# Router logits taken from the raw residual beside the output projection, and roots ahead of the first modulation, in a two-layer mixture-of-experts trunk on one Trainium2 core

## The chip, the core and the metric

The kernel runs on one core of a Trainium2 chip (trn2). The metric is the device time of one execution in microseconds, less is better. Three runs of the kernel before are shown, and one execution was profiled.

## The reference

Two layers work on 384 tokens of 1024 features (128 context tokens of one request, 256 latent tokens of another), all in float32. Cut to what the change touches, each layer computes:

```python
sh1, sc1, gt1, sh2, sc2, gt2 = ada_mod(cond, w_ada[l], b_ada[l])   # silu(cond) @ w_ada + b_ada, per request
h = rms_norm(y, g_attn[l]) * (1 + sc1) + sh1                       # first modulation
...                                                               # three attention groups on h @ w_in
y = y + gt1 * (o @ w_out[l])                                       # output projection, residual y
h = rms_norm(y, g_ffn[l]) * (1 + sc2) + sh2                        # second modulation
scores = sigmoid(h @ w_router)                                     # 16 experts in 4 groups
# best group by the sum of its top 2 of scores + b_router, top 2 experts inside it, weights normalised
y = y + gt2 * moe(h, ...)                                          # gate, up, silu, down for the chosen experts
```

`rms_norm(y, g)` is y times its root 1/sqrt(mean(y*y) + 1e-6), times g. The root is one number per token, so `h @ w_router` equals root * (y @ (g (1+sc2) w_router)) + sh2 @ w_router. `cond` is one vector for the context tokens and one for the latent tokens, so gain and shift have two sets of columns.

## The kernel before

The five engines each run one hand-written program (TensorE from line 724, ScalarE from 1163, VectorE from 1438, GpSimd from 1887, the SyncE transfers from 578); semaphores join them. The residual lies transposed in `zT` (features on partitions, 8 blocks k of 384 tokens), the modulated input in `hT`. Products are float32, and each shows in the trace as two matmul records. PSUM has 8 banks: six go round for "jobs" in the order of `job_order` (L156), bank 7 (`bN`) holds the sums of squares, banks 6 and 7 the attention outputs.

**Order of the work around the change, layer 0 start.** TensorE turns the input rows, adds the squares with 48 records of one column (`piece_sums`, L736), and goes on to the four adaLN chunks of the first modulation (`ada`, L787: a job A is a product of 32 columns wide tiles over a 2 MB weight chunk, L795, a job B turns the row that ScalarE copied out, L802). Beside that, VectorE works out the root by three Newton steps (`rsqrt`, L1465). Then TensorE spreads the root over a bank (`spread`, L763, job n1b), and VectorE normalises: for each block k one product with the spread root (L1521), and for odd k the modulation too (L1516); ScalarE modulates the even blocks (`modulate`, L1196, record L1202). The projection cq0 (L829) waits for each block in turn (`h_ready`, L751), and all products of the layer follow.

**The end of attention.** The output projection has eight jobs op0 to op7 of 8 products each (`proj`, L807, record L813), queued without a gap. VectorE adds each to the residual (L1677), ScalarE squares it (L1194), VectorE adds the squares (L1671). Then TensorE runs job A of the first of the chunks in `ADA_ROUTE[l]` (four in layer 0, two in layer 1), the sums (L748), A of the second, B of the first, the spread of the root (job n2b), and the router: 8 products of 32 columns wide tiles, each waiting for its block of `hT` (L1006). ScalarE copies the logits out, TensorE turns them (L1013), VectorE reduces them (L1720), ScalarE takes the exponential (L1331), and VectorE chooses group and experts in a chain of small operations (L1723 to L1732, ends with `s_mask`), then works out weights (L1737 to L1749). TensorE turns `hT` back into rows (jobs hr00 to hr21, L1009 and L1017, record L733), ScalarE copies them out and stores them to `hscr` (L1336), runs jobs A and B of the chunks that are left, waits for `s_mask`, and ranks the tokens (L1024 to L1030). VectorE reads the rank (L1752), makes one-hot matrices (L1782), TensorE makes slots with them (L1046), GpSimd gathers rows of `hscr` (L1970), and the experts begin.

In layer 0 two chunks stand behind the turns (A and B of the third around the mask, the fourth behind the rank, L1032), in layer 1 only one job B.

**The experts.** Each of 16 takes three 2 MB weight chunks from a ring of six slots; SyncE loads a slot when its last reader is done (L661).

Of the kernel before, what the change touches and what calls it, by code (L numbers as in the profile page):

```python
# [15 lines left out]
P = 128  # L16
# [139 lines left out]
def job_order():  # L156

    order = ["vecA", "vecB"] + [f"x{t}{h}" for t in range(NT) for h in range(2)]
    for l in range(DEPTH):
        n = (ada_jobs(ADA_FIRST) if l == 0 else []) + ["n1b"] + (BETWEEN_SPREAD if l else [])  # L160
        n += ["cq0"] + (BETWEEN_FIRST if l else []) + ["cq1"] + [f"nav{t}" for t in range(NT)] + ["ckv", "kpe", "swk"] + [f"swv{t}" for t in range(NT)]
        n += ["nqc", "naq0", "nkc", "naq1", "nqb", "nak0", "nkb", "nak1", "rkp", "swq0", "cache1", "cache2", "swq1", "swq2"]
        n += ["mq0", "mq1", "mq2", "mq3", "rm0", "mq4", "mq5", "rm1", "mk0", "mk1", "rm2", "mk2", "mk3", "mk4", "mk5"]
        for i in range(NS + LAG_PV):
            if i < NS:
                n.append(f"S{i}")
            n += ENTRY.get(i, [])
# [12 lines left out]
    order += ["nfb"] + [f"fo{t}{h}" for h in range(2) for t in range(NT)]  # L180
    at, signalled, busy, where = 0, [0] * NB, [None] * NB, {}
    for j in order:
        wide = j[1] in PAIRED if type(j) is tuple else False
        if wide:
            at += at % 2
        b = at % NB
        taken = [b, b + 1] if wide else [b]
        before = {busy[k] for k in taken if busy[k] is not None}
        where[j] = (b, signalled[b], sorted(before))
        signalled[b] += 1  # L190
        for k in taken:
            busy[k] = (b, signalled[b])
        at += len(taken)
    return where
# [44 lines left out]
def build(nc, A, C_dram, O):  # L239
    with ExitStack() as ctx:  # L240
        def sb(name, shape, dt=F32):
            return ctx.enter_context(nc.sbuf_tensor(name, shape, dt))
# [35 lines left out]
        gcol = sb("gcol", [P, 2])  # L278
        wqb = sb("wqb", [P, 2, MH * QKD])
# [66 lines left out]
        wr32 = c3(carve(KT * 32), KT)  # L346
# [25 lines left out]
        bN = banks[7]  # L372
        bX, bG, bU, bA, bY = banks[0:2], banks[2], banks[3], banks[4], banks[5:7]
# [42 lines left out]
        s_wr = sem("s_wr")  # L416
        s_rexp = sem("s_rexp")
# [307 lines left out]
        def _(pe):  # L725
# [25 lines left out]
            def h_ready(l, which, k):  # L751

                pe.wait_ge((s_ha, s_hv)[k % 2], 4 * norm_no(l, which) + k // 2 + 1)
# [30 lines left out]
            pe.wait_ge(s_sil, 1)  # L784

            for l in range(DEPTH):
# [20 lines left out]
                def proj(name, w, c, m, first_after=None):  # L807

                    b = fill_begin((l, name))
                    for k in range(KT):  # L810
                        if first_after is not None:
                            h_ready(l, first_after, k)
                        last = mm(b[0:m, 0:T], w[:, k, c:c + m], hT[:, k, :], start=(k == 0), stop=(k == KT - 1))  # L813
                    filled((l, name), last)
# [14 lines left out]
                proj("cq0", w, NAH * HD, P, first_after=0)  # L829
# [169 lines left out]
                if l == 0:  # L999
                    pe.wait_ge(s_bs, 16 * 4)  # L1000

                pe.wait_ge(s_wr, 2 * (l + 1))
# [152 lines left out]
            for h in range(2):  # L1155
                if h == 0:
                    pe.wait_ge(s_hv, 4 * norm_no(DEPTH, 0) + 1)
                else:
                    read_out(pe, "nfb")
                for t in range(NT):  # L1160
                    turn4(f"fo{t}{h}", lambda k: hT[:, 4 * h + k, t * P:(t + 1) * P])

        @block.scalar
        def _(act):
# [31 lines left out]
            def modulate(l, which):  # L1196

                for k in range(0, KT, 2):
                    act.wait_ge(s_xn, 4 * norm_no(l, which) + k // 2 + 1)
                    for cond in range(2):  # L1200
                        x = hT[:, k, sel(cond)]
                        last = A_(x, x, ACT.Identity, bias=modT[:, l, 24 * which + k, cond:cond + 1],  # L1202
                                  scale=gain[:, which, k, cond:cond + 1])
                    last.then_inc(s_ha, 1)
# [11 lines left out]
            for l in range(DEPTH):  # L1216
# [4 lines left out]
                modulate(l, 0)  # L1221
# [217 lines left out]
        def _(v):  # L1439
# [62 lines left out]
            def gains(l, which):  # L1502
# [4 lines left out]
                chain(tt(gain[:, which], gain[:, which], g, ALU.mult))  # L1507

            def normalise(j, l, which):

                b = take(v, j)

                def modulate(k):
                    for cond in range(2):
                        x = hT[:, k, sel(cond)]
                        ins = ts(x, x, gain[:, which, k, cond:cond + 1], modT[:, l, 24 * which + k, cond:cond + 1],  # L1516
                                 ALU.mult, ALU.add)
                    ins.then_inc(s_hv, 1)

                for k in range(KT):  # L1520
# [8 lines left out]
                    if k % 2:  # L1529
                        modulate(k)  # L1530
# [10 lines left out]
            for l in range(DEPTH):  # L1541
# [4 lines left out]
                for j in ada_jobs(ADA_FIRST) if l == 0 else []:  # L1546
                    ada(l, j)

                v.wait_ge(s_mod, len(ADA_FIRST if l == 0 else ADA_FIRST + ADA_ATT))
                gains(l, 0)  # L1550
                normalise((l, "n1b"), l, 0)
# [120 lines left out]

                for n in range(KT):
# [9 lines left out]
                v.wait_ge(s_mod, ADA_ALL.index((0, 9) if l == 0 else (1, 7)) + 1)  # L1683
                gains(l, 1)
                add_squares(KT - 1)
                rsqrt((l, 1), D)
                for j in route[0:3]:
                    ada(l, j)
                normalise((l, "n2b"), l, 1)


# [23 lines left out]

                b = take(v, (l, "routerT"))
                if l + 1 < DEPTH:

                    v.wait_ge(s_bmw, 16 * (l + 2))
                evac((l, "routerT"), nc.vector.tensor_reduce(  # L1720
                    te(R[0]), b[:, 0:T].rearrange("p (t g r) -> p t r g", t=NT, g=4)[:, :, 0:NE, :], AX.X, ALU.add))
# [166 lines left out]
        def _(g):  # L1888
# [30 lines left out]
            for l in range(DEPTH):  # L1919
# [35 lines left out]
                nc.gpsimd.memset(wr32[:, :, NE:32], 0.0).then_inc(s_wr, 1)  # L1955
                nc.gpsimd.tensor_copy(wr32[:, :, 0:NE], wr[:]).then_inc(s_wr, 1)
# [64 lines left out]
```

## Time and profile before

| | |
|---|---|
| runs shown | 1251.38, 1252.31, 1255.2 us, median 1252.31 |
| profiled execution | 1255.41 us, its span 1253.4 us (2.01 us lie around the span) |
| mean granted TensorE clock of the profiled execution | 0.947 |
| TensorE busy | 1152.9 us, 92% of the span |
| VectorE, ScalarE, GpSimd busy | 772.4, 632.9, 127.8 us |
| moved by DMA | 314.35 MB, mean 251 GB/s |

A row of the timeline gives the start in us from the span's start, the time it took, engine, line of the kernel, operation, output<-input with shapes, and a count; in brackets stands how long the engine was idle before and what released it. PEld is the weight load of TensorE. A row of a table by stage gives, for a stretch, its length and each engine's busy time and number of records in it, the granted clock (1.00 is the full clock), the busy share of the DMA engines and what they moved. In a chain row stand start, length and what lay on the chain.

### The profile page before, as it was taken

The numbers are of one execution on the slowest core, as the hardware profiler recorded it, in microseconds if no ns is written. First come the engines' busy times: TensorE is split into PE (matmuls) and PEld (weight loads), VectorE is DVE, ScalarE is ACT, GpSimd is POOL, SyncE is SP. The second block draws the span as 40 slices with busy tenths as digits, with TensorE's granted clock in tenths as the row PEclk, the third lists the DMA queues.
The fourth block names the chain that finished last, engine by engine and source line by source line (L and its number), as shares of the span: only waits on it lengthen the run. The fifth ranks groups of instructions, "written<-read, shape, count | busy, mean of one in ns | idle before, by whom it ended". The sixth has DMA issues, their size and how long they took to land.

```text
span 1253.4 us, 14864 instructions
## 1 busy us (share of the span) xinstructions
PE 1152.9 (92%) x5574; PEld 844.6 (67%) x5574; DVE 772.4 (62%) x1056; ACT 632.9 (50%) x751; POOL 127.8 (10%) x157
## 2 busy tenths in 40 slices
PE   6999998897899999999879998889789999999956
PEld 5576354554788888888666754455578888888846
DVE  1312356427698888888451233742768888988845
ACT  2201455315377777777320035631447777777721
POOL 2241100310100101010010011000000101010000
PEclk9899999999799999999969998999779999999985
DMA  9994478339489999999699140002549999999621
GB/s 330 335 309 169 145 264 280 100 109 377 148 321 372 359 376 366 383 375 367 221 345 240 68 168 16 1 1 81 245 158 352 369 375 378 377 364 369 257 87 75
DMA packets 81257, 314.35 MB, mean 251 GB/s; under 512 B 22766, under 2 KB 27100, under 8 KB 68396
## 3 DMA queue, kind: packets, MB, share of 16 engines
q1 hardware_dynamic: 65548, 279.17, 61.2%
q0 software_dynamic: 13152, 24.96, 6.0%
q10 hardware_dynamic: 2496, 9.44, 2.0%
q8 instruction: 35, 0.57, 0.2%
q14 instruction: 26, 0.21, 0.1%
HBM read 308.11 MB, written 26.38 MB: 267 GB/s over the span
## 4 chain that ended last, share of the span: by engine, by line
PE 84%; DVE 7%; issue 3%; ACT 3%; DMA 2%; SPq 0%; ACTq 0%; POOL 0%; POOLq 0%; DVEq 0%
PE bank L813 17%; PE bank L1072 14%; PE bank L1066 14%; PE bank L1067 14%; PE bank L795 3%; PE bank L941 3%; PE bank L820 3%; PE bank L740 2%; PE bank L1056 2%; PE bank L955 2%; ACT work L1295 2%; PE bank L733 2%; PE bank L973 1%; PE bank L1046 1%; PE bank L874 1%
## 5 line engine op out<-in xcount | busy, mean ns | idle before, releaser
L1791 DVE TENSOR_TENSOR ring_r<-ring,work_r 128x4096 fp32r<-128x4096 f32 x96 | 421.6, 4416 | 0.1
L1352 ACT ACTIVATE work_r<-ring 128x4096 fp32r<-128x4096 f32 x96 | 349.6, 3644 | 138.0 <-PE bank L1067 104.4
L1066 PE MATMUL bank<-work_r 128*128 128x512 f32 x768 | 310.1, 404 | 12.3 <-issue 5.1
L1067 PE MATMUL bank<-work_r 128*128 128x512 f32 x768 | 303.9, 396 | 0.0
L813 PE MATMUL bank<-hT,ring 128*128 128x384 f32 (+1 forms) x640 | 213.7, 493 | 3.3 <-ACT hT L1202 1.9
L1072 PE MATMUL bank<-ring_r,work_r 128*128 128x512 f32 x768 | 195.1, 396 | 0.4 <-DVE ring_r L1791 0.4
L813 PEld LDWEIGHTS bank<-hT,ring 128*128 128x128 f32 (+1 forms) x640 | 121.5, 192 | 88.0 <-issue 11.6
L1066 PEld LDWEIGHTS bank<-work_r 128*128 128x128 f32 x768 | 147.5, 192 | 43.9 <-issue 5.8
L1072 PEld LDWEIGHTS bank<-ring_r,work_r 128*128 128x128 f32 x768 | 144.2, 188 | 34.5 <-DVE ring_r L1791 0.8
L1067 PEld LDWEIGHTS bank<-work_r 128*128 128x128 f32 x768 | 147.1, 192 | 29.6
L1174 ACT ACTIVATE work<-bank 128x384 f32<-128x384 f32 (+6 forms) x79 | 38.0, 494 | 179.7 <-PE bank L813 89.3
L1970 POOL DMA_INDIRECT work<-hscr,idxg x32 | 32.8, 1026 | 402.7 <-PE bank L1056 260.9
L1625 DVE TENSOR_REDUCE st<-bank 128x2 f32<-128x768 f32 (+1 forms) x48 | 37.4, 778 | 50.3 <-PE bank L941 40.6
L1977 POOL DMA_INDIRECT yscr<-work,idxs x32 | 32.1, 1004 | 276.5 <-ACT work L1378 276.5
L795 PE MATMUL bank<-ring,sil 128*32 128x512 f32 x384 | 50.8, 655 | 7.4 <-ACT work L1295 5.6
L1796 DVE TENSOR_TENSOR work_r<-bank,work_r 128x512 fp32r<-128x512 f32 x64 | 41.2, 685 | 26.6 <-ACT work_r L1359 26.6
L1295 ACT ACTIVATE work<-bank,st 128x384 f32<-128x384 f32 (+1 forms) x96 | 47.9, 506 | 17.3 <-DVE st L1625 9.5
L1677 DVE SCALAR_TENSOR_TENSOR zT<-bank,modT,zT 128x256 f32<-128x256 f32 (+1 forms) x32 | 11.9, 413 | 67.9 <-PE bank L813 67.9
L941 PE MATMUL bank<-work 64*128 64x384 f32 (+3 forms) x192 | 48.0, 467 | 6.1 <-ACT work L1295 4.7
L1194 ACT ACTIVATE work<-zT 128x384 f32<-128x384 f32 x16 | 8.4, 523 | 80.6 <-DVE zT L1677 80.6
L955 PE MATMUL bank<-cst,work 128*128 128x128 f32 x224 | 35.2, 288 | 12.3 <-ACT work L1295 8.9
L1810 DVE TENSOR_TENSOR work_r<-bank,work_r 128x512 fp32r<-128x512 f32 x32 | 22.1, 691 | 37.8 <-ACT work_r L1371 37.8
(202 smaller groups left out, 1152.7 us busy)
## 6 DMA issues: line engine op xcount, KB each, us to landing
ring<-in_w_gate SPq DMA_DIRECT2D x32, 2048.0 KB, 11.5
ring<-in_w_up SPq DMA_DIRECT2D x32, 2048.0 KB, 12.3
ring<-in_w_down SPq DMA_DIRECT2D x32, 2048.0 KB, 12.3
ring<-in_w_ada SPq DMA_DIRECT2D x24, 2048.0 KB, 10.0
ring<-in_w_in SPq DMA_DIRECT2D x4, 2048.0 KB, 15.5
work<-yscr ACTq DMA_DIRECT2D x6, 1024.0 KB, 7.1
ring<-in_w_out SPq DMA_DIRECT2D x4, 1280.0 KB, 8.0
ring<-in_w_in SPq DMA_DIRECT2D x12, 256.0 KB, 6.9
```

The source lines that it names most:

```text
L795: last = mm(b[32 * (k % 4):32 * (k % 4) + 32, :], sil32[:, k, :], w[:, k, :], start=(k < 4), stop=(k >= 4), skip_group_check=True)
L813: last = mm(b[0:m, 0:T], w[:, k, c:c + m], hT[:, k, :], start=(k == 0), stop=(k == KT - 1))
L941: last = mm(b[:, s, 0:n], lhs, rhs, start=True, stop=True)
L955: last = turn_(b[:, s, c * P:(c + 1) * P], pr[(2 * i + s) % 6][:, c * P:(c + 1) * P], ident)
L1066: mm(b[:], x_hi[:, k, :], hi[:, k, half, :], start=(k == 0), stop=False)
L1067: last = mm(b[:], x_lo[:, k, :], hi[:, k, half, :], start=False, stop=False)
L1072: last = mm(b[:], x_hi[:, k, :], lo[:, k, half, :], start=False, stop=(k == nk - 1))
L1174: evac(j, A_(dst, src, ACT.Copy, scale=scale))
L1295: ins = A_(pr[(2 * i + s) % 6][:, 0:n], b[:, s], ACT.Exp, bias=st[:, r, 0, s:s + 1], accum_out=st[:, r, 1, s:s + 1])
L1352: A_(w_hi[:, slot % 2, :], ring[slot][:], ACT.Copy).then_inc(s_hi, 1)
L1791: tt(ring_r[slot][:], ring[slot][:], w_hi[:, slot % 2, :].bitcast(F32), ALU.subtract).then_inc(s_lo, 1)
L1796: ins = tt(xs_lo[:, 4 * h:4 * h + 4, :], bX[h][:].rearrange("p (k s) -> p k s", k=4), xs_hi[:, 4 * h:4 * h + 4, :].bitcast(F32), ALU.subtract)
```

## The change

The first spread of layer 0 moves ahead of its four adaLN chunks; VectorE multiplies all eight blocks by the spread root then, and modulation alone is left for after the chunks. In each layer, gain 2 is worked out before the output projection, two weight sets `wz` (gain times router weights, one per condition) are made by VectorE, and TensorE accumulates `wz` times the raw residual block n-1 behind job op n, the last one behind the first adaLN product. Eight tiny products of the shift with the router weights (`wb`) give a bias, which ScalarE adds when it copies the logits out. VectorE multiplies by the root after the turn and the reduction. ScalarE modulates all eight blocks of the second modulation, VectorE only normalises them; the turn of the logits moves ahead of B of the first chunk and of the spread, and all six turns of `hT` come behind.

```diff
 job_order:
-        n = (ada_jobs(ADA_FIRST) if l == 0 else []) + ["n1b"] + (BETWEEN_SPREAD if l else [])
+        n = ["n1b"] + (BETWEEN_SPREAD if l else ada_jobs(ADA_FIRST))
-        n += r[0:3] + ["n2b", "router", "hr00", "routerT"] + [f"hr{t}{h}" for t in range(NT) for h in range(2)][1:]
+        n += r[0:2] + ["routerT"] + r[2:3] + ["n2b"] + [f"hr{t}{h}" for t in range(NT) for h in range(2)]
 TensorE:
-            pe.wait_ge(s_sil, 1)
...
-                for j in ada_jobs(ADA_FIRST) if l == 0 else []:
-                    ada(j)
                 spread((l, "n1b"), roots_before(l, 0) + 1)
-                for j in BETWEEN_SPREAD if l else []:
+                if l == 0:
+                    pe.wait_ge(s_sil, 1)
+                for j in BETWEEN_SPREAD if l else ada_jobs(ADA_FIRST):
                     ada(j)
...
+                def router_part(k):
+                    read_out(pe, (l, f"op{k}"))
+                    for cond in range(2):
+                        c = sel(cond)
+                        last = mm(bR[32 * (k % 4):32 * (k % 4) + 32, c], wz[:, k, cond, :], zT[:, k, c], start=(k < 4 and cond == 0), stop=(k >= 4),
+                                  skip_group_check=True)
+                    return last
                 for n in range(KT):
...
                     proj(f"op{n}", w, (n % 4) * P, P)
+                    if n == 0:
+                        if l == 0:
+                            pe.wait_ge(s_bs, 16 * 4)
+                        pe.wait_ge(s_wr, 3 * (l + 1))
+                        for k in range(KT):
+                            last = mm(bN[32 * (k % 4):32 * (k % 4) + 32, 8:10], wb[:, k, :], modT[:, l, 24 + k, :], start=(k < 4),
+                                      stop=(k >= 4), skip_group_check=True)
+                        last.then_inc(s_router, 1)
+                        pe.wait_ge(s_wz, l + 1)
+                    else:
+                        router_part(n - 1)
                 for j in route[0:1]:
                     ada(j)
+                router_part(KT - 1).then_inc(s_router, 1)
+                pe.wait_ge(s_rlog, 2 * l + 1)
                 sums_of_added(l)
-                for j in route[1:3]:
+                for j in route[1:2]:
                     ada(j)
-                spread((l, "n2b"), roots_before(l, 1) + 1)
...
-                b = fill_begin((l, "router"))
-                for k in range(KT):
-                    h_ready(l, 1, k)
-                    last = mm(b[32 * (k % 4):32 * (k % 4) + 32, 0:T], wr32[:, k, :], hT[:, k, :], start=(k < 4), stop=(k >= 4),
-                              skip_group_check=True)
-                filled((l, "router"), last)
-                turn4((l, "hr00"), lambda k: hT[:, k, 0:P])
-                read_out(pe, (l, "router"))
+                pe.wait_ge(s_rlog, 2 * (l + 1))
                 b = fill_begin((l, "routerT"))
...
-                for i in range(1, 2 * NT):
+                for j in route[2:3]:
+                    ada(j)
+                spread((l, "n2b"), roots_before(l, 1) + 1)
+                for i in range(2 * NT):
                     t, h = divmod(i, 2)
+                    pe.wait_ge(s_ha, (4 + KT) * l + 4 + 4 * (h + 1))
                     turn4((l, f"hr{t}{h}"), lambda k: hT[:, 4 * h + k, t * P:(t + 1) * P])
 ScalarE:
+                act.wait_ge(s_router, 2 * l + 1)
+                A_(rbias[:], bN[:, 8:10], ACT.Copy).then_inc(s_rlog, 1)
                 squares_behind_out(l)
-                for j in route[0:3]:
+                for j in route[0:1]:
                     ada_row(l, j)
-                modulate(l, 1)
...
-                copy((l, "router"), rlog, T)
-                read_out(act, (l, "routerT"))
+                act.wait_ge(s_router, 2 * l + 2)
+                for cond in range(2):
+                    last = A_(rlog[:, sel(cond)], bR[:, sel(cond)], ACT.Identity, bias=rbias[:, cond:cond + 1])
+                last.then_inc(s_rlog, 1)
+                for j in route[1:3]:
+                    ada_row(l, j)
+                act.wait_ge(s_logit, l + 1)
                 A_(rw[:, 0, :], rw[:, 0, :], ACT.Exp, scale=-1.0).then_inc(s_rexp, 1)
+                modulate_all(l)
 VectorE, layer 0 start:
+                    normalise_first((l, "n1b"))
+                    for j in ada_jobs(ADA_FIRST):
+                        ada(l, j)
+                    v.wait_ge(s_mod, len(ADA_FIRST))
+                    gains(l, 0).then_inc(s_xn, 4)
+                    v.wait_ge(s_xn, 4)
+                    read_out(v, (l, "n1b"))
+                    for k in range(1, KT, 2):
+                        modulate(l, 0, k)
 VectorE, before op0:
+                chain(gains(l, 1))
+                v.wait_ge(s_bs, 16 * 4)
+                for cond in range(2):
+                    ins = tt(wz[:, :, cond, 0:NE], wr[:], gain[:, 1, :, cond].unsqueeze(2).to_broadcast([P, KT, NE]), ALU.mult)
+                ins.then_inc(s_wz, 1)
 VectorE, behind the root:
+                for j in route[0:2]:
+                    ada(l, j)
...
+                    both_parts, b[:, 0:T].rearrange("p (t g r) -> p t r g", t=NT, g=4), AX.X, ALU.add))
+                read_out(v, (l, "routerT"))
+                v.wait_ge(s_root, roots_before(l, 1) + 1)
+                chain(tt(te(R[0]), both_parts[:, :, 0:NE], ns[:, 1, :].unsqueeze(2).to_broadcast([P, NT, NE]), ALU.mult))
+                tt(te(R[0]), te(R[0]), both_parts[:, :, NE:2 * NE], ALU.add).then_inc(s_logit, 1)
+                for j in route[2:3]:
+                    ada(l, j)
+                normalise_second((l, "n2b"))
                 v.wait_ge(s_rexp, l + 1)
 GpSimd:
-                nc.gpsimd.memset(wr32[:, :, NE:32], 0.0).then_inc(s_wr, 1)
-                nc.gpsimd.tensor_copy(wr32[:, :, 0:NE], wr[:]).then_inc(s_wr, 1)
+                nc.gpsimd.memset(wz[:, :, :, NE:32], 0.0).then_inc(s_wr, 1)
+                nc.gpsimd.memset(wb[:, :, 0:NE], 0.0).then_inc(s_wr, 1)
+                nc.gpsimd.tensor_copy(wb[:, :, NE:32], wr[:]).then_inc(s_wr, 1)
```

`normalise_second` is eight products of `zT` and the spread root on VectorE, each released to ScalarE; `modulate_all` is the two modulations of each of the eight blocks on ScalarE; `modulate(l, 0, k)` on VectorE is the two of one odd block.

## Rows read from the trace of the kernel before

**Rows 1.** The page: the chain that ended last, shares of the span by engine.

```profile
PE 84%; DVE 7%; issue 3%; ACT 3%; DMA 2%; SPq 0%; ACTq 0%; POOL 0%; POOLq 0%; DVEq 0%
```

**Rows 2.** Table by stage: output projection of layer 1, idle ahead of rank, rank, start of cq0.

```profile
833.20:874.70 41.50, 41.48 (x128) 24.28 (x129) 7.52 (x19) 3.66 (x7) 0.49 (x2) 1.00 0.14 51
892.55:895.88 3.33, 0.00 (x0) 0.00 (x0) 2.92 (x14) 2.46 (x5) 0.00 (x0) 0.96 0.89 359
895.90:899.90 4.00, 4.00 (x18) 3.91 (x18) 3.62 (x16) 4.00 (x2) 0.00 (x0) 0.50 0.22 89
45.00:48.80 3.80, 3.80 (x7) 2.02 (x6) 2.77 (x8) 1.97 (x4) 0.00 (x0) 0.50 1.05 388
```

**Rows 3.** Timeline of the start of layer 0.

```profile
12.61 3.68 PE L733 MATMUL bank<-cst,work 128*128 128x128 f32 x16 [0.64 <-DMA work<-in_x_sample]
16.81 3.21 ACT L1185 ACTIVATE hT<-zT 128x512 f32<-128x512 f32 x6
17.49 10.40 PE L740 MATMUL bank<-cst,hT 128*128 128x1 f32 x48 [1.20 <-ACT hT L1185]
28.03 0.16 DVE L1473 TENSOR_SCALAR ns<-bank 128x3 f32<-128x3 f32 x1 [11.88 <-PE bank L740]
30.29 0.17 DVE L1485 SCALAR_TENSOR_TENSOR ns<-ns 128x3 f32<-128x3 f32 x1
39.68 0.66 PE L802 MATMUL bank<-cst,arow 128*128 128x128 f32 x4 [0.69 <-ACT arow L1174]
41.22 1.02 DVE L1521 TENSOR_TENSOR hT<-zT,bank 128x384 f32<-128x384 f32 x2
42.94 13.61 PE L813 MATMUL bank<-hT,ring 128*128 128x384 f32 x32 [1.93 <-ACT hT L1202]
```

**Rows 4.** The chain of waits at the start of layer 0.

```profile
27.89 5.64 PE bank L795 x32
33.53 0.59 PE bank L802 x4
34.12 1.85 PE bank L795 x16
```

**Rows 5.** Timeline of layer 1, from op7 to the first gather.

```profile
874.70 1.92 PE L795 MATMUL bank<-ring,sil 128*32 128x512 f32 x16
876.96 0.83 PE L748 MATMUL bank<-cst,work 128*128 128x1 f32 x6 [0.34 <-DVE work L1671]
880.30 0.93 PE L768 MATMUL bank<-cst,ns 128*128 128x128 f32 x6
889.74 2.35 PE L733 MATMUL bank<-cst,hT 128*128 128x128 f32 x20
890.61 0.19 DVE L1723 TENSOR_SCALAR work<-work 128x48 f32<-128x48 f32 x1 [0.31 <-ACT work L1331]
895.89 0.61 PE L1027 MATMUL bank<-work,cst 128*128 128x16 f32 x2 [3.37 <-DVE work L1732]
904.90 1.34 POOL L1970 DMA_INDIRECT work<-hscr,idxg  x1 [71.06 <-issue]
```

**Rows 6.** Timeline of layer 0: first job A, rank, first one-hot.

```profile
280.14 1.93 PE L795 MATMUL bank<-ring,sil 128*32 128x512 f32 x16
301.39 0.40 PE L1027 MATMUL bank<-work,cst 128*128 128x16 f32 x2 [1.37 <-DVE work L1732]
307.70 3.69 DVE L1782 TENSOR_TENSOR work_r<-cst,work 128x512 fp32r<-128x512 f32 x6
```

**Rows 7.** Timeline of ScalarE in layer 1: a modulated block, the last store of rows.

```profile
886.75 0.99 ACT L1202 ACTIVATE hT<-hT,modT,gain 128x256 f32<-128x256 f32 x2 [0.64 <-DVE hT L1521]
894.59 0.33 ACTq L1336 DMA_DIRECT2D hscr<-work  x1
```

**Rows 8.** Table by stage: 14 experts of layer 1.

```profile
943.26:1194.42 251.16, 251.16 (x1178) 208.78 (x1177) 220.79 (x113) 193.72 (x126) 26.25 (x26) 1.00 0.93 352
```

**Rows 9.** The line of the six stores to `hscr`: time from issue to landing.

```profile
DMA to landing us min/median/max: 2.7/3.6/11.0
```

More of the change, by code:

```diff
@@ L416, in build @@
         s_wr = sem("s_wr")
+        s_wz = sem("s_wz")
+        s_router = sem("s_router")
+        s_rlog = sem("s_rlog")
+        s_logit = sem("s_logit")
         s_rexp = sem("s_rexp")
@@ L749, in sums_of_added, with h_ready @@
                 last.then_inc(s_sum, 1)
-            def h_ready(l, which, k):
-                pe.wait_ge((s_ha, s_hv)[k % 2], 4 * norm_no(l, which) + k // 2 + 1)
+            def h_ready(l, k):
+                pe.wait_ge((s_ha, s_hv)[k % 2], ((4 + KT) * l, 4 * l)[k % 2] + k // 2 + 1)
             def sums(j, sq, nk):
@@ L805, in _, with proj @@
                 route = ada_jobs(ADA_ROUTE[l])
-                def proj(name, w, c, m, first_after=None):
+                def proj(name, w, c, m, paced=False):
                     b = fill_begin((l, name))
                     for k in range(KT):
-                        if first_after is not None:
-                            h_ready(l, first_after, k)
+                        if paced:
+                            h_ready(l, k)
                         last = mm(b[0:m, 0:T], w[:, k, c:c + m], hT[:, k, :], start=(k == 0), stop=(k == KT - 1))
@@ L1194, in squares_behind_out, with modulate_block, modulate_even, modulate_all @@
                     A_(sq_new[n % 2] if n else sq_sum, zT[:, n, :], ACT.Square).then_inc(s_sq, 1)
-            def modulate(l, which):
-                for k in range(0, KT, 2):
[L1199 to L1204, printed above, removed]
+            def modulate_block(l, which, k):
+                for cond in range(2):
+                    x = hT[:, k, sel(cond)]
+                    last = A_(x, x, ACT.Identity, bias=modT[:, l, 24 * which + k, cond:cond + 1],
+                              scale=gain[:, which, k, cond:cond + 1])
+                last.then_inc(s_ha, 1)
+            def modulate_even(l):
+                for k in range(0, KT, 2):
+                    act.wait_ge(s_xn, (4 + KT - 1) * l + k // 2 + 1)
+                    modulate_block(l, 0, k)
+            def modulate_all(l):
+                for k in range(KT):
+                    if k < KT - 1:
+                        act.wait_ge(s_xn, (4 + KT - 1) * l + 4 + k + 1)
+                    else:
+                        read_out(act, (l, "n2b"))
+                    modulate_block(l, 1, k)
             def ada_row(l, j):
@@ L1506, in gains, with modulate, normalise_first, normalise_second @@
                 chain(ts(gain[:, which], modT[:, l, 24 * which + 8:24 * which + 16, :], 1.0, None, ALU.add))
-                chain(tt(gain[:, which], gain[:, which], g, ALU.mult))
+                return tt(gain[:, which], gain[:, which], g, ALU.mult)
+            def modulate(l, which, k):
+                for cond in range(2):
+                    x = hT[:, k, sel(cond)]
+                    ins = ts(x, x, gain[:, which, k, cond:cond + 1], modT[:, l, 24 * which + k, cond:cond + 1],
+                             ALU.mult, ALU.add)
+                ins.then_inc(s_hv, 1)
+            def normalise_first(j):
+                b = take(v, j)
+                for k in range(KT):
+                    ins = tt(hT[:, k, :], zT[:, k, :], b[:, 0:T], ALU.mult)
+                evac(j, ins)
+            def normalise_second(j):
+                b = take(v, j)
+                for k in range(KT):
+                    ins = tt(hT[:, k, :], zT[:, k, :], b[:, 0:T], ALU.mult)
+                    if k < KT - 1:
+                        ins.then_inc(s_xn, 1)
+                evac(j, ins)
             def normalise(j, l, which):
                 b = take(v, j)
[L1513 to L1518, printed above, removed]
                 for k in range(KT):
@@ L1529, in normalise @@
                     if k % 2:
-                        modulate(k)
+                        modulate(l, which, k)
             def normalise_last(j):
@@ L1545, in _ @@
                     ada(l, j)
[L1546 to L1551, printed above, removed]
+                if l == 0:
+                    normalise_first((l, "n1b"))
[7 more added lines that the diff above has]
+                        modulate(l, 0, k)
+                else:
+                    v.wait_ge(s_mod, len(ADA_FIRST + ADA_ATT))
+                    chain(gains(l, 0))
+                    normalise((l, "n1b"), l, 0)
                 for i in range(2):
@@ L1671, in add_squares @@
                     tt(sq_sum, sq_sum, sq_new[n % 2], ALU.add).then_inc(s_sqadd, 1)
+                v.wait_ge(s_mod, ADA_ALL.index((0, 9) if l == 0 else (1, 7)) + 1)
+                chain(gains(l, 1))
+                v.wait_ge(s_bs, 16 * 4)
+                for cond in range(2):
+                    ins = tt(wz[:, :, cond, 0:NE], wr[:], gain[:, 1, :, cond].unsqueeze(2).to_broadcast([P, KT, NE]), ALU.mult)
+                ins.then_inc(s_wz, 1)
                 for n in range(KT):
```

21 lines of the change are left out of this document (8 added, 13 removed).

## The prediction

> **What bounds the kernel now.** I read the page's chain first, then tables by stage, then the timeline around the two places that the change touches. The chain is 84% TensorE [rows 1], so what counts is when TensorE is held back or given more. In the output projection it is busy 41.48 of 41.50 us, 128 records of 384 columns, 0.324 us each [rows 2]: whatever is put there is paid in full. In the experts it is busy all of 251.16 us [rows 8], so a late start of the experts is a late end. Between these lie the two latency-bound stretches: the start of layer 0 [rows 3, 4], and in each layer the stretch from op7 to the one-hot matrices [rows 5, 6], where the path hops from engine to engine. A time worked out for a stretch is counted from E, the end of op7, which before is 874.70 in layer 1 and 280.14 in layer 0.
>
> **Start of layer 0.** The root is moved ahead of four adaLN chunks. Before, TensorE leaves the sums at 27.89 [rows 3] and starts the first job A at once [rows 4], while VectorE needs 2.43 us for the root, from 28.03 to 30.46 [rows 3]. After, the spread stands ahead of the first A, so TensorE stands still until 30.52: +2.63 us. The spread itself (0.93 us warm [rows 5]) comes off nothing, because before it lay beside the wait for the last B's modulation; at the half rate seen there it is up to 1.4: +0.9 to +1.4. Behind the last B, the path to cq0 was 2.60 us, from 40.34 to 42.94 [rows 3]; it loses one normalising product of 0.55: −0.55. The other seven were already hidden: cq0 ran at the clock of 0.50 [rows 2], seven records in 3.8 us, 1.1 us a block, slower than ScalarE gives blocks out (0.99 for each second one [rows 7]), so that having all blocks normalised buys nothing more. The eight products (8 x 0.51 = 4.1 us [rows 3]) run beside the first two A jobs (5.64 us [rows 4]). Sum: +3.2, bounds +2.4 (the clock rises earlier because the spread comes first) and +4.
>
> **In the output projection.** Removed is the router behind the normalisation; it was paced by the blocks, not by its own time. Added are seven parts ahead of op7's end, each 2 conditions x 2 records over 256 and 128 columns. By the 0.324 us for 384 columns [rows 2] a part is 0.65 us of streaming. They use 32 columns of the array, and the neighbours use 128. No row shows a narrow product amid wide ones in this stage; the nearest are jobs A and B in turn. A (16 records of 512 columns, four tiles at once) would stream in 1.73 by the same rate and takes 1.85; B (4 of 128 columns) would in 0.43 and takes 0.59 [rows 4]. So a change of shape costs at most 0.12 to 0.16 us, a part 0.65 to 0.97; I take 0.8. The Trainium skill ("TensorEngine Tiling (Array Packing)", Key Properties) says that changing the tiling mode drains the array; it gives no time. If all of A's and B's excess is that, a part costs 0.97 and the forecast goes up by 2.4 us over both layers; without a drain it goes down by 2.1. The bias adds 16 records of two columns. Nearest is the sums row, six records in 0.83 [rows 5], 0.14 each with wide weights, thus at most 2.2; four tiles at a time it would be a quarter, 0.5: I take 1.0. The memsets of GpSimd and the two products for `wz` on VectorE come within op0 (16 records, 5.2 us) and cost nothing; were they late, the bias and the whole rest of the projection would stand behind them. Each part reads block n-1, which VectorE has added by then (it needs under 1 us of the 5.2). Per layer E moves by 7 x 0.8 + 1.0 = **+6.6 us**, bounds +5.0 and +9.0.
>
> **From op7 to the mask.** After, with rows 5 for the times: A to E+2.0, last part to 2.8, sums to 3.6 (squares were ready before), root to 6.1; on TensorE the second A to 5.6, ScalarE's two copies of the logits are done beside it, three turns to 6.1, B to 6.8, spread to 7.7. VectorE reduces and scales the logits before that, then normalises 8 x 0.51 = 4.1 us to E+11.8 and starts the chain of choices there. Before, it started at 890.61, E+15.9. This is the gain: −4.1, less than the 6.6 above. The chain takes 5.3 us (890.61 to 895.89), so the mask is there at E+17.1 instead of E+21.2.
>
> **What is late next.** The turns of `hT` stand on TensorE ahead of the rank, and now wait for ScalarE alone. It starts its first block at E+8.3. One block is 0.99 [rows 7]; in a stream ScalarE hides some of it (six squares in 3.21, 0.54 each, against 0.62 alone), so I take 0.9 for a block, bounds 0.85 and 0.99: done at E+15.5. hr00 needs four blocks, the other five need all. TensorE has then done nothing but four short records for 7.8 us. Before, an idle stretch of 3.33 us was enough for the clock to stand at 0.50 in the rank [rows 2]. A turn at the low rate is 0.23 (16 in 3.68 [rows 3]), at the full one 0.12 (20 in 2.35 [rows 5]). I take the low one: five turns of four are 4.6 us, to E+20.1.
> - Layer 1: one B (0.7) puts the rank at E+20.8 instead of E+21.2 (895.89−874.70), −0.4. VectorE's weights wait for the same B, so nothing there is sooner. All of the mask's gain is gone.
> - Layer 0: A and B lie between. A is 1.85 at full and 3.79 at half rate (5.64−1.85 [rows 4]), the clock rising somewhere in it: 2.8; with B 0.7 the rank starts at E+23.6 instead of E+21.25 (301.39−280.14 [rows 6]), +2.3. Behind the rank everything keeps its 6.3 us to the first one-hot (301.39 to 307.70).
>
> Stores to `hscr`: ScalarE copies behind the turns and issues the last at about E+20.7, before at E+19.9 [rows 7]. It may land 11 us later [rows 9]; the first gather is at E+30.2 in layer 1 [rows 5] where the landings are the shorter ones. Hidden, with 1 to 6 us to spare. SyncE's loads that wait for the moved A jobs come up to 3 us later in layer 0; their data is wanted by the second expert: nothing.
>
> **Sum:** 3.2 + 2 x 6.6 + 2.3 − 0.4 = **+18.3 us**. The profiled execution would go from 1255.41 to 1273.7; it lies 3.1 above the median 1252.31, and against that the forecast is **1270.6 us**.
>
> **Rivals.**
> - *Turns at the full clock.* hr00 and the light work keep the clock up, as the paced router did before. Turns end at E+17.9, rank at E+18.6 in layer 1 (−2.6) and E+20.5 in layer 0 (−0.8): 3.2 + 13.2 − 3.4 = +13.0, 1265.3. For it: the clock stayed up with a product pair in each 1.6 us; against: here are 4 and 3 us with nothing.
> - *The mask decides.* If ScalarE's blocks come at the pace of VectorE's (0.51), the turns are done before the mask, and each layer gains the whole 4.1: 3.2 + 13.2 − 8.2 = +8.2, 1260.5. Against: no row shows ScalarE that fast.
> - *The experts give it back* (not slower). If the weight stream bounds the experts and is not itself late, the delay of both layers up to the experts disappears, and only the start's 3.2 is left: 1255.5, within what counts as no change. The transfers are busy 0.93 at 352 GB/s there, TensorE 1.00 [rows 8]; it decides once the transfers are the busier of the two. Against: SyncE loads a slot only when TensorE has read it, so a late start is late for the stream too.
> - *Parts dearer*: 0.97 a part, 2.2 for the bias, gives E+9.0: 1275.4. It is the top of the forecast's own range.
> - *The change does not do what it says* would show as logits taken after normalisation; the program's order leaves no room for it.
>
> **Chances.** Forecast (with dear parts in it) 0.58, full clock 0.22, mask 0.08, experts 0.05; the rest is for things unseen, more of it above no change than below. The range takes in the first two and their bounds: from 1260 (full clock with parts of 0.65, 0.5 for the bias and +2.4 at the start: 1252.3+9.0, less 1 for a mask that decides in one layer) to 1278 (+4 at the start, E+9.0 twice, blocks of 0.99 and a slow A that put the ranks at +4.0 and +0.3: +26.3). A difference of under 0.3% (3.8 us) can't be told from none: slower 0.91, same 0.06, faster 0.03.
>
> **What would show it.** In the profile after: TensorE idle 2.6 us ahead of the spread at 27.9; cq0 starts near 46. The output projection takes 48 us instead of 41.5 up to the first A. VectorE starts the choices about 12 us behind op7 and 4 us sooner relative to it. ScalarE modulates without a pause for 7.2 us. The turns take 4.6 us at a clock of 0.50, and the rank's releaser is TensorE's own order, not VectorE's mask. It is wrong if a part takes under 0.4 us, if cq0 starts by 44, or if the experts' stage gets shorter.

## The result and the profile after

The changed kernel takes 1266.6 us (median of 4 runs, 1265.89 to 1269.0); four runs of the kernel before gave a median of 1251.85 us. The ratio is 1.0116, 95% interval 1.0096 to 1.0136: 14.5 us slower, between 12.0 and 17.0. The forecast was +18.3 us, 1270.6, with a range of 1260 to 1278: the time lies in the range, the +18.3 above the measured interval.

The page after has a span of 1265.0 us, 11.6 more than before; the chain's line, against [rows 1]:

```profile
PE 85%; DVE 6%; ACT 4%; issue 3%; DMA 2%; SPq 0%; ACTq 0%; POOL 0%; DVEq 0%; POOLq 0%
```

In rounded shares VectorE lost a point of the chain, and TensorE and ScalarE gained one each, which is the change in small. The table by stage after (columns as in [rows 2]): output projection of layer 1 up to the end of op7; one job of it with its part; the wait for ScalarE's blocks in layer 1; the turns in layer 0 and in layer 1.

```profile
839.25:886.95 47.70, 47.70 (x168) 26.02 (x168) 8.22 (x23) 3.83 (x8) 0.78 (x3) 1.00 0.12 45
243.22:249.35 6.13, 6.13 (x22) 3.32 (x21) 1.28 (x4) 0.69 (x2) 5.19 (x9) 1.00 0.45 108
894.94:902.10 7.16, 1.12 (x4) 0.72 (x4) 6.75 (x20) 7.16 (x17) 0.00 (x0) 0.73 1.01 435
300.43:304.70 4.27, 4.27 (x24) 4.10 (x28) 1.03 (x6) 2.62 (x5) 0.00 (x0) 0.54 0.61 250
902.12:905.90 3.78, 3.78 (x22) 3.78 (x23) 1.02 (x6) 2.21 (x4) 0.00 (x0) 0.61 0.67 276
```

The first row answers to 41.50 us in [rows 2]: TensorE is as busy as it was, for 6.2 us longer. The last three show ScalarE busy without a pause while TensorE has 1.12 us of work, and then turns at a clock of 0.54 and 0.61.

Timeline after, start of layer 0, against [rows 3]:

```profile
16.47 9.39 PE L747 MATMUL bank<-cst,hT 128*128 128x1 f32 x48 [1.21 <-ACT hT L1205]
28.48 1.65 PE L775 MATMUL bank<-cst,ns 128*128 128x128 f32 x6 [2.62 <-DVE ns L1525]
30.06 5.91 PE L800 MATMUL bank<-ring,sil 128*32 128x512 f32 x32
43.74 3.61 ACT L1220 ACTIVATE hT<-hT,modT,gain 128x256 f32<-128x256 f32 x8 [1.67 <-DVE gain L1547]
44.87 7.41 PE L818 MATMUL bank<-hT,ring 128*128 128x384 f32 x17 [2.08 <-ACT hT L1220]
```

The sums end at 25.86 in this execution (27.89 before; that is ahead of anything that was changed), then come 2.62 us of idle time. Timeline after, layer 1, against [rows 5]: second A, turn of the logits, start of the choices, the turns, rank, first one-hot.

```profile
890.66 1.92 PE L800 MATMUL bank<-ring,sil 128*32 128x512 f32 x16
892.51 0.55 PE L1029 MATMUL bank<-cst,work 128*128 128x128 f32 x3
894.36 3.80 DVE L1568 TENSOR_TENSOR hT<-zT,bank 128x384 f32<-128x384 f32 x8
894.94 7.12 ACT L1220 ACTIVATE hT<-hT,modT,gain 128x256 f32<-128x256 f32 x16 [0.53 <-DVE hT L1568]
898.07 0.19 DVE L1797 TENSOR_SCALAR work<-work 128x48 f32<-128x48 f32 x1
902.12 3.83 PE L740 MATMUL bank<-cst,hT 128*128 128x128 f32 x20 [2.39 <-ACT hT L1220]
906.22 0.29 PE L1047 MATMUL bank<-work,cst 128*128 128x16 f32 x2
909.70 3.70 DVE L1856 TENSOR_TENSOR work_r<-cst,work 128x512 fp32r<-128x512 f32 x6
```

op7 ends at 886.95 here. The choices start 11.1 us behind it, 4.8 sooner than before. The rank starts 19.3 us behind it, only 1.9 sooner: it stands behind the turns, and these behind ScalarE. In layer 0 (op7 ends at 285.26) the rank starts at 307.00, 21.7 us behind, 0.5 later than before.

Stretch by stretch, after minus before, each read from the two timelines: before the sums' end −2.0; start of layer 0 to cq0's end +2.6; from there to op0 −1.7; op0 to op7 +6.2; op7 to first one-hot, layer 0, +0.4; from there to op0 of layer 1 +0.5; op0 to op7 +6.2; op7 to one-hot, layer 1, −1.6; the rest +0.9. That is 11.6, the difference of the spans. The −1.7 is not of the change: from cq0's end to op0 it took 187.2 us in before, e1, e2, e4 and e9 and 185.6 in after, e3, e5 to e8, e10 and e11, with and without each part of the change. The granted clock tells the two apart. In the five of 187.2 it stands at its lower level once in this stretch; in the others it does not. Table by stage, before:

```profile
154.92:158.33 3.41, 3.41 (x18) 0.60 (x16) 1.78 (x4) 1.23 (x4) 1.20 (x3) 0.50 0.64 235
```

In 3.41 us at half the full clock TensorE does the work of 1.7, and the other 1.7 are the difference. The five stretches that it touches add up to +13.9 (2.6+6.2+0.4+6.2−1.6, of unrounded rows), inside the measured interval of 12.0 to 17.0.

### The profile page after: what moved, and what is told of

It is laid out like the page before. It is cut to its first block, busy times and chain, and to the rows that moved or that the text cites. A ratio compares the mean times of both kernels' runs of the same rounds, so it can differ in the third digit from the quotient of the medians.

```text
span 1265.0 us, 15023 instructions
## 1 busy us (share of the span) xinstructions
PE 1158.2 (92%) x5638; PEld 847.8 (67%) x5638; DVE 763.8 (60%) x1048; ACT 640.6 (51%) x771; POOL 128.4 (10%) x159
## 4 chain that ended last, share of the span: by engine, by line
PE 85%; DVE 6%; ACT 4%; issue 3%; DMA 2%; SPq 0%; ACTq 0%; POOL 0%; DVEq 0%; POOLq 0%
PE bank L818 17%; PE bank L1092 14%; PE bank L1086 14%; PE bank L1087 13%; PE bank L800 3%; PE bank L946 3%; PE bank L825 2%; PE bank L747 2%; PE bank L1076 2%; PE bank L960 2%; PE bank L740 2%; ACT work L1328 2%; PE bank L978 1%; DVE ring_r L1865 1%; PE bank L1066 1%
## 6 DMA issues: line engine op xcount, KB each, us to landing
ring<-in_w_up SPq DMA_DIRECT2D x32, 2048.0 KB, 11.6
ring<-in_w_down SPq DMA_DIRECT2D x32, 2048.0 KB, 11.8
```

## The experiments

Eleven kernels ran, each compared with the kernel before on its chip. Differences below are the ratio's, times 1252.3. Each has an interval of about ±2 to ±5 us (given with the ratio), and one kernel's difference from another a wider one; the rows are of one profiled execution of each.

**e1, the old start with the rest of the change.** `job_order`, TensorE's and VectorE's programs at the start of layer 0 put back.

```diff
-                spread((l, "n1b"), roots_before(l, 0) + 1)
                 if l == 0:
                     pe.wait_ge(s_sil, 1)
-                for j in BETWEEN_SPREAD if l else ada_jobs(ADA_FIRST):
+                for j in ada_jobs(ADA_FIRST) if l == 0 else []:
+                    ada(j)
+                spread((l, "n1b"), roots_before(l, 0) + 1)
+                for j in BETWEEN_SPREAD if l else []:
                     ada(j)
```

> The changed kernel with only the start of layer 0 put back (adaLN chunks ahead of the spread, normalising behind them). Theory (TensorE stands idle 2.6 us for the root and gets almost nothing back): about 2.6 us faster than the changed kernel, that is +12 us against the kernel before. Rival (the start is paid back by the modulation that is left alone): no difference from the changed kernel, +14.7 us.

Ratio 1.0089 (1.0061 to 1.0117): +11.1 us, 3.4 less than the changed kernel. The two intervals overlap, so the 3.4 alone does not show the price. From the sums' end to cq0's end it takes 23.5 us, as before (23.5), against 26.1. Its chain shows why little more is to be had there:

```profile
15.94 20.04 DMA ring<-in_w_ada
36.02 1.92 PE bank L800 x16
```

In this execution TensorE stood idle 1.54 us until the fourth adaLN chunk had landed, which it did not in before.

**e2, the new start alone.** The same lines changed in the kernel before.

> The kernel before with only the start of layer 0 changed. Theory: 2.6 us slower than before (ratio 1.002), TensorE idle 2.6 us ahead of the spread, cq0's start 17.5 to 19 us behind the end of the sums instead of 15.05. Rival: within 1 us of before.

Ratio 1.0009 (0.9988 to 1.003), an interval that holds both 0 and +2.6, so the time alone does not tell. The trace does: sums' end to cq0's end is 26.3 us, 2.8 more than before. By time e6 against e4 (below) gives 2.5 us, but no pair that differs in the start is clear of zero by itself.

Over all profiled executions the stretch took 22.6 to 23.5 us with the old start and 25.9 to 26.3 with the new one, but for e3: it has the new start and took 23.0. There cq0 ran at the full clock throughout, in 5.4 us instead of 7.1 to 8.5. So the moment at which the clock rises in an execution can hide the price.

**e3, each part issued twice.**

```diff
                 def router_part(k):
                     read_out(pe, (l, f"op{k}"))
+                    pe.wait_ge(s_rlog, 2 * l + 1)
                     for cond in range(2):
                         c = sel(cond)
+                        mm(bN[32 * (k % 4):32 * (k % 4) + 32, 128 + c.start:128 + c.stop], wz[:, k, cond, :], zT[:, k, c],
+                           start=False, stop=True, skip_group_check=True)
```

> The changed kernel with each router part issued twice, the first time into spare columns of bank 7. Theory (a part is 0.65 us of streaming, and the remaining 0.3 of its 0.97 us is paid for changing between 32 and 128 columns): the second part has no change of shape and adds 0.65 us, so a job of the projection comes each 6.78 us instead of 6.13, in all 16 x 0.65 = 10.4 us above the changed kernel. Rival (a part streams at a lower rate, no price for the change of shape): 7.1 us for each job, 15.5 us above.

Ratio 1.0181 (1.0143 to 1.0219): +22.7 us, 8.2 above the changed kernel where 10.4 were expected. A job of the projection with its two parts, in the table by stage:

```profile
240.15:246.92 6.77, 6.77 (x25) 3.75 (x25) 1.29 (x4) 1.22 (x3) 5.18 (x9) 1.00 0.42 98
```

A plain job is 5.16 us, with one part 6.13, with two 6.77. The first part costs 0.97, the second 0.64, which is its streaming time. So 0.33 us of each part is paid once for coming between wide products, whatever follows it in the same shape; the rival's 7.1 us a job is refuted. That the price is for going from 128 columns to 32 and back is the nearest reading; no run put short products of 128 columns there to compare. The page "TensorEngine Tiling (Array Packing)" of the Trainium skill (Key Properties) says that a change of mode drains the array; the two rows agree with it, and 0.33 us would be its size here.

**e4, all parts in one run.**

```diff
                         pe.wait_ge(s_wz, l + 1)
-                    else:
-                        router_part(n - 1)
                 for j in route[0:1]:
                     ada(j)
+                for k in range(KT - 1):
+                    router_part(k)
                 router_part(KT - 1).then_inc(s_router, 1)
```

> The changed kernel with all eight router parts in one run behind the first adaLN product, none between the jobs of the projection. Theory (TensorE's time beside the projection is the price; neighbouring parts lie on different groups of 32 columns and run together): the projection is back to 41.8 us (bias 0.4), the run of eight takes 1.5 to 3 us instead of one part's 0.8, so per layer 3.5 to 5 us less, in all 7 to 10 us less than the changed kernel, +5 to +8 against before. Rival (parts don't overlap, eight cost 5.2 to 6.2 us wherever they are): no more than 2 us less.

Ratio 1.0008 (0.9993 to 1.0023): +1.0 us, 13.5 less than the changed kernel. Timeline of layer 1:

```profile
873.95 1.92 PE L800 MATMUL bank<-ring,sil 128*32 128x512 f32 x16
875.69 1.54 PE L998 MATMUL bank<-zT,work 128*32 128x256 f32 x32
```

All 32 records take 1.54 us, where between the jobs four took 0.97. Neighbouring parts write different groups of 32 columns, and run four at a time; the neighbours A and the run have one shape. op0 to op7 is 41.9 us. In rows this saves 5.8 us a layer in the projection, less about 1.0 in layer 0 and 0.5 in layer 1 behind it: 10 us, the top of the 7 to 10 expected. The time shows 13.5, and the trace has more too: from the first product of an expert in layer 0 to op0 of layer 1, where the kernels are the same, e4 took 505.1 us and the changed kernel 509.3. Tables by stage of that stretch, the changed kernel and e4:

```profile
329.99:839.25 509.26, 481.60 (x2318) 361.33 (x2319) 334.92 (x381) 288.12 (x333) 40.37 (x46) 0.95 0.70 253
326.99:832.04 505.05, 476.87 (x2319) 358.60 (x2319) 334.94 (x381) 288.02 (x333) 40.35 (x46) 0.97 0.70 255
```

The work is the same, the granted clock is not (0.95 and 0.97). It is so in all 13 profiled executions: the stretch took 503.7 to 505.1 us at a mean clock of 0.97 (e2, e4, e8) and 507.3 to 509.8 at 0.95 or 0.96 (the ten others, before with 508.7). Why the clock stood lower for longer in some is not shown. A difference of a few us between two executions that lies in this stretch can't be put down to the change in the code.

**e8, TensorE kept at work ahead of the turns.** Eleven products whose result nobody reads.

```diff
                 spread((l, "n2b"), roots_before(l, 1) + 1)
+                for _ in range(11):
+                    mm(bR[:, 0:T], ident, zT[:, 0, :], start=True, stop=True)
```

> The changed kernel with 11 more products of 384 columns into bank 6 behind the spread, ahead of the turns; their result is not read. Theory (TensorE's clock is at its lower level in the turns because TensorE stands idle ahead of them): granted clock 1.00 in the turns, five turns in 2.4 us instead of 4.3 and 3.8; the rank starts 1.5 to 2 us sooner behind op7 in each layer, 3 to 4 us less than the changed kernel. Rival (the low clock has another cause): turns stay at 3.8 to 4.3 us and the time does not change.

Ratio 1.0052 (1.0032 to 1.0072): +6.5 us, 8.0 less than the changed kernel, with more work. Table by stage, the turns in layer 0 and in layer 1:

```profile
300.05:302.45 2.40, 2.40 (x24) 2.23 (x28) 1.02 (x6) 1.70 (x4) 0.00 (x0) 1.00 0.68 278
893.44:895.84 2.40, 2.40 (x22) 2.40 (x23) 1.02 (x6) 1.71 (x4) 0.00 (x0) 1.00 0.70 294
```

2.40 us at a clock of 1.00, against 4.27 at 0.54 and 3.78 at 0.61. TensorE's clock in the turns was its lower level because of the idle time ahead, as the forecast had it. The rank starts 1.9 and 1.4 us sooner behind op7; the first expert's product 2.7 and 1.3. That is 4 of the 8.0 us, and as much as was expected (3 to 4). The rest is not explained: this execution had the short 503.7 us in the stretch named above, but it was also 2.2 us under the median of its kernel.

**e5, the adaLN jobs ahead of the turns.** TensorE's lines; ScalarE copies the two rows behind its second and fifth block, VectorE reduces them earlier.

```diff
                 spread((l, "n2b"), roots_before(l, 1) + 1)
+                for j in route[3:]:
+                    ada(j)
                 for i in range(2 * NT):
-                    t, h = divmod(i, 2)
+                    h, t = divmod(i, NT)
...
-                for j in route[3:5]:
-                    ada(j)
                 pe.wait_ge(s_mask, l + 1)
...
-                for j in route[5:]:
-                    ada(j)
```

> The changed kernel with the adaLN jobs that stood behind the turns of hT put ahead of them (A, B, A, B, B in layer 0, one B in layer 1), ScalarE copying their rows between its blocks, and the turns of the first half blocks ahead of those of the second. Theory (behind the logits the path is ScalarE's blocks, then TensorE's turns, then what TensorE has queued between them and the one-hot matrices; the jobs fit into TensorE's idle 8 us): layer 0 comes to its first one-hot about 21.4 us behind op7 instead of 27.95, layer 1 about 21 instead of 22.75: 8.5 us less than the changed kernel, +6 against before. Rival (VectorE's chain of choices, weights and rank sets the end): under 3 us less.

Ratio 1.0055 (1.0035 to 1.0075): +6.9 us, 7.6 less than the changed kernel. The one-hot matrices come 20.3 and 19.6 us behind op7 instead of 27.95 and 22.75, sooner than expected. The edit does two things at once there: it takes the jobs out of the way, and it fills TensorE's idle time ahead of the turns, which in layer 0 ran at a granted clock of 1.00 (297 to 302 us). How much each of the two gave is not separated. But in layer 0 the first expert's product came 42.5 us behind op7, only 2.3 us sooner. The chain of layer 0 names what is late next:

```profile
305.23 12.38 DMA hscr<-work
318.42 4.38 DMA work<-hscr,idxg
```

The last store of rows took over 12 us, beside two weight loads of 2 MB which SyncE issues as soon as the early chunks are read (at 294.0 and 296.5); the changed kernel's stores took 4.2 us at most. One load is enough: in before and in e8 the last store of layer 0 was issued 0.6 and 0.2 us behind a load and took 11.0 and 11.5 us, in the changed kernel 1.2 us ahead of the load, and took 3.8.

**e6, old start and parts in one run**, e1 and e4 together.

> The changed kernel with the old start of layer 0 and all parts in one run behind the first adaLN product. Theory (the price of the new start is 2.6 us and stands by itself): 2.6 us less than e4_parts_together, so about -1.6 against before (ratio 0.9987). Rival (the start costs nothing): as e4_parts_together, +1.0.

Ratio 0.9988 (0.9972 to 1.0003): −1.5 us, 2.5 less than e4, as expected (2.6), though the two intervals overlap.

**e7, e6 and e5 together.**

> e6_old_start_together and e5_chunks_early in one: early logits at a low price and the work behind them in TensorE's idle time. Theory: the gains add, -1.6 - 8.5 = -10 against before, 1243 us. Rival (the stores of rows land late, or the experts start no sooner): no better than -4.

Ratio 0.9964 (0.9949 to 0.9978): −4.5 us, faster than the kernel before but not by the 10 expected. The rival's mechanism is in the trace: the store landed 11.85 us after its issue, and the first gather of layer 0 waited for it (first two rows); in e9 it did not, but its data was late then (last row).

**e9, loads held until the rows have landed**, from e7.

```diff
                             is_filled(sp, last_reader(l, MOE_AT[l] - SLOTS + slot))
+                            if l == 0 and slot in (4, 5):
+                                sp.wait_ge(s_hscr, 16 * NT)
```

> e7_all_three, with SyncE's two weight loads that follow the last two adaLN chunks of layer 0 held until the rows of hscr have landed. In e7_all_three the last store of rows took 12 us to land there, beside these loads. Theory (the loads crowd the stores, and the first gather waits for them): the store lands in about 4 us, the first gather starts about 6 us sooner, the first expert's product 5 to 6 us sooner behind op7: 5 us less than e7_all_three, ratio 0.992. Rival (the landing takes that long by itself, or the held weights are then missed): no less than e7_all_three, ratio 0.996 or more.

Ratio 0.9938 (0.9914 to 0.9962): −7.8 us, 3.3 less than e7 where 5 were expected; the intervals overlap, so the trace has to tell. Timelines of e7 and, in the second fence, of e9:

```profile
296.57 0.33 ACTq L1380 DMA_DIRECT2D hscr<-work  x1
309.24 2.73 POOL L2037 DMA_INDIRECT work<-hscr,idxg  x1 [57.12 <-DMA hscr<-work]
```

```profile
299.07 0.33 ACTq L1382 DMA_DIRECT2D hscr<-work  x1
302.69 0.33 SPq L668 DMA_DIRECT2D ring<-in_w_down  x1
304.93 1.31 POOL L2039 DMA_INDIRECT work<-hscr,idxg  x1 [50.44 <-DVE gsl L1844]
315.38 1.97 PE L1078 MATMUL bank<-cst,work 128*128 128x128 f32 x8 [3.98 <-DMA work<-hscr,idxg]
```

With no load beside them the stores landed within 3.6 us (load released at 302.69), and the gather was issued when its indices were there. Then it took 10.4 us to land, beside the released loads (5.0 in e7). The product came 41.5 us behind op7 instead of 42.9; 5 to 6 had been expected.

**e10, e9 with unread products in layer 1** (8 ahead of the first group of turns, 4 ahead of the second).

> e9_loads_held, with 8 and 4 unread products of 384 columns into bank 6 ahead of the two groups of turns in layer 1 alone. Theory (TensorE idles there, and its clock is at the lower level in turns and rank): rank and first one-hot 1 to 1.5 us sooner in layer 1, 1 to 1.5 us less in all. Rival: the products delay the turns and nothing is gained.

Ratio 0.9934 (0.9916 to 0.9951), no difference from e9 that the time can show. In the trace the first one-hot of layer 1 comes 20.1 us behind op7 instead of 21.0, the first product 36.1 instead of 37.8.

**e11, loads held until two gathers have landed**, from e10.

```diff
-                                sp.wait_ge(s_hscr, 16 * NT)
+                                sp.wait_ge(s_g[0], 16)
+                                sp.wait_ge(s_g[1], 16)
```

> e10_held_filler, with the two weight loads of layer 0 held until the first two gathers have landed instead of the stores of rows. In e9_loads_held the gathers were issued at 304.9 and the turn of their tokens still waited 4.0 us for them, beside the loads released at 302.7. Theory (the same crowding, one step later): the wait ahead of the first tokens' turn goes, the first expert's product comes about 37.5 us behind op7 in layer 0 instead of 41.9, 3 to 4 us less, ratio 0.990. Rival (the weights held longer are then missed by the first experts): time as e10_held_filler, ratio 0.9934, and a wait for ring transfers among the first experts.

Ratio 0.9916 (0.99 to 0.9933): −10.5 us, 1241.3 us, faster than both kernels. By time that is 2.2 us less than e10, not clear of zero (3 to 4 expected). Timeline of layer 0:

```profile
304.77 1.02 POOL L2043 DMA_INDIRECT work<-hscr,idxg  x1 [0.31 <-issue]
308.95 0.33 SPq L668 DMA_DIRECT2D ring<-in_w_down  x1
309.50 1.97 PE L1082 MATMUL bank<-cst,work 128*128 128x128 f32 x8
314.01 0.76 PE L1092 MATMUL bank<-work_r 128*128 128x512 f32 x1 [2.54 <-issue]
```

The first gather landed 3.5 us after its issue at 303.2, TensorE no longer waits for it, and the first product is 37.3 us behind op7 (37.5 expected), 4.6 sooner than in e10 and 7 sooner than in before (44.3).

One question is left untested. The order of the adaLN jobs, the held loads and the unread products could be put into the kernel before, without the early logits. No run did that, so what part of the −10.5 us the early logits earn is not shown.

## Why the prediction was right, and where it was off

The sign and its cause held. +18.3 was 3.8 too many: the measured time is inside the range, but the rival with the turns at the full clock (+13.0) is nearer to +14.5 by its number alone. It is the rows that decide for the forecast's mechanism. Point by point:

- **Start of layer 0**: forecast +3.2, rows +2.6 (e2: +2.8), by time 1.1 (e2), 2.5 (e4 to e6) and 3.4 us (e1), none clear of zero alone. The idle stretch is 2.62, forecast 2.63. The spread took 1.65, above the forecast's 1.4. What comes back through the clock was mis-sized: in this execution cq0 got the full clock sooner (from 44.87 to about 52.0, 7.1 us instead of 8.5), in e2 the first two A jobs did (4.9 instead of 5.7). It is partly luck: e1 has the old start and also a cq0 of 7.1.
- **In the output projection**: forecast +6.6 up to op7, rows +6.2. The total is near because errors met. A part is 0.97 and not 0.8: the bound from jobs A and B was right and the value inside it was not. The bias is 0.43 (5.59 for op0 with it) and not 1.0: its 16 records show 0.31 us. And I counted seven parts ahead of op7, where the order has six; the part of block 6 stands behind it: 6 x 0.97 + 0.43 = 6.25. With the part at 0.97, the reading by the drain of the Trainium skill ("TensorEngine Tiling (Array Packing)", Key Properties) was the better of the two.
- **Op7 to the mask**: the choices start at E+11.1, forecast 11.8. VectorE's eight products take 3.80 in a run, less than 8 x 0.51, the rate of the pairs in [rows 3].
- **What is late next**: as forecast, ScalarE's blocks (7.12 us; 7.2), then turns at the lower clock (4.29 and 3.83; 4.6), and the mask's gain lost in them. The mask is done 16.4 us behind op7 in both layers, the rank starts at 21.7 and 19.3. That the idle time ahead brings the low clock, and the clock its share of the delay, is shown by e8; e5 shows that jobs moved out of the way bring the one-hot matrices forward, with a higher clock mixed in.
- **The term that was off most**: layer 0 behind the turns, forecast +2.3, rows +0.4. I let the job A behind the turns run at the lower clock for half its length. It took 1.86 us (304.65 to 306.51), as at the full clock, 0.9 less than the 2.8 forecast. The turns ended 0.7 sooner than forecast and B took 0.2 less; these three make up the difference. In layer 1 the forecast was −0.4 and the rows say −1.6, again with turns that ended 1.3 us sooner than forecast and a B of 0.44 instead of 0.7.
- **The rivals**: full clock in the turns fell (0.54 and 0.61). The mask did not decide (16.4 against 19.3 and 21.7). The experts gave nothing back: from first one-hot of layer 0 to op0 of layer 1 it is +0.5 us.
- The forecast for `hscr` (hidden) held for this change; e5 shows how close it was, because the loads that crowd the stores follow the adaLN jobs, and e8, where a load came 0.2 us ahead of the last store.

## What to carry to other kernels

Work put into a stretch where an engine is busy without a gap is paid in full; count it before the latency that it takes off a path elsewhere. Narrow products belong in one run with others of their shape, on different column groups: eight took 1.5 us so, and 0.97 us each scattered among wide ones. When a result is brought forward, follow every engine to the next joint: here the early logits brought no gain even with the parts in one run (+1.0 us, e4), and the largest gain came with changes to the order of TensorE's queue, its clock and the transfers beside the stores. And when two traces differ where the code does not, look at the granted clock of that stretch first.

## What the runs showed of the hardware that was not expected

- A part between wide products costs 0.33 us beyond its streaming, and a second one behind it does not (6.13 and 6.77 us a job, e3).
- Eight parts in one run over four column groups take 1.54 us, against 0.97 us for one between wide products (e4).
- Sixteen records of two columns over four column groups take 0.31 us together, and 0.43 us of the job that they stand in.
- Rows of 512 KB stored from ScalarE's queue landed in 2.6 to 4.2 us in the changed kernel and in e9, but in 11.4 to 12.4 when two loads of 2 MB had been issued on SyncE's 6 to 11 us before (e5, e7), and in 11.0 and 11.5 behind one issued 0.6 and 0.2 us before (before, e8). A gather issued 2.2 us behind such a load held up TensorE for 4.0 us (e9).
- The same code, from the first expert of layer 0 to op0 of layer 1, took 503.7 to 505.1 us at a mean granted clock of 0.97 and 507.3 to 509.8 at 0.95 or 0.96.
- A useless product can be worth its time: 11 of them ahead of the turns brought these from 4.27 to 2.40 us (e8).
